# Splitting the tokens 256 and 288 in the output and down products, with one 512-column matmul for the high and low operand

## The reference

```python
def hybrid_layer(h, pos, states, p):
    u = rms_norm(h, p['norm_mix']) @ p['w_in']
    ...
    mixed = jnp.concatenate([y_ssd, y_ret, y_gla, y_lru], axis=-1) @ p['w_out']   # 1024 -> 1024
    h = h + mixed.astype(h.dtype)
    hn = rms_norm(h, p['norm_ffn'])
    h = h + ((jax.nn.silu(hn @ p['w_gate']) * (hn @ p['w_up'])) @ p['w_down']).astype(h.dtype)   # 2816 -> 1024
    return h, ...
```

## Time and profile before

| | |
|---|---|
| median of 3 runs | 1333.41 us |
| span of the profiled execution | 1330.0 us |
| TensorE matmul busy | 1298.5 us (98%), 10781 matmuls |
| TensorE weight load busy | 1248.2 us (94%), 10781 loads |
| VectorE busy | 856.3 us (64%) |
| ScalarE busy | 707.0 us (53%) |
| GpSimd busy | 293.9 us (22%) |

### The profile page before, as it was taken

One profiled execution on the slowest core, in us unless ns is written; L12 is line 12 of the kernel. 1 busy time (PEld: TensorE's weight loads), 2 busy tenths in 40 slices (PEclk: granted clock), 3 DMA queues, 4 the chain that ended last, 5 costly groups with the idle time before them and its releaser, 6 DMA issues.

```text
span 1330.0 us, 26928 instructions
## 1 busy us (share of the span) xinstructions
PE 1298.5 (98%) x10781; PEld 1248.2 (94%) x10781; DVE 856.3 (64%) x1697; ACT 707.0 (53%) x1209; POOL 293.9 (22%) x248
## 2 busy tenths in 40 slices
PE   7999999999999999999999999999999999999996
PEld 7988898999999999999998878889999999999996
DVE  5844766478853785378757547755788348834863
ACT  7625464666642674266663264556676247624641
POOL 1100100112243224324411010001123412341250
PEclk9999989999999999999999999999999999999997
DMA  8846745567744784476566566447477347835741
GB/s 269 212 102 143 163 109 122 109 143 166 173 129 104 171 170 128 104 171 170 145 143 156 114 151 160 96 113 161 103 170 188 111 104 169 190 109 104 169 125 68
DMA packets 63387, 189.73 MB, mean 143 GB/s; under 512 B 7584, under 2 KB 8864, under 8 KB 63264
## 3 DMA queue, kind: packets, MB, share of 16 engines
q0 software_dynamic: 27936, 67.12, 30.7%
q1 hardware_dynamic: 30672, 111.95, 26.7%
q10 hardware_dynamic: 4656, 8.95, 2.2%
HBM read 180.33 MB, written 5.43 MB: 140 GB/s over the span
## 4 chain that ended last, share of the span: by engine, by line
PE 79%; DVE 9%; ACT 4%; DVEq 3%; DMA 2%; issue 2%; ACTq 0%; SPq 0%
PE bank L1622 41%; PE bank L1651 31%; DVE ct L975 1%; DMA raw<-weights 1%; PE bank L1565 1%; DVE lru_x L975 1%; PE bank L1939 1%; ACT wl L540 1%; ACT wh L541 1%; DMA wl<-weights 1%; DVE up L1495 0%; PE bank L1583 0%; DVEq L974 0%; PE bank L1945 0%; DMA h<-x 0%
## 5 line engine op out<-in xcount | busy, mean ns | idle before, releaser
L512 POOL DMA_DIRECT2D wl<-weights x194 | 168.5, 869 | 892.4 <-ACT wl L540 880.3
L1622 PE MATMUL bank<-xh,wh 128*128 128x272 f32 x800 | 243.4, 304 | 8.1 <-DVE xl L930 7.7
L541 ACT ACTIVATE wh<-raw 128x512 fp32r<-128x512 f32 (+1 forms) x243 | 197.7, 815 | 89.0 <-PE bank L1622 79.2
L1622 PE MATMUL bank<-xh,wl 128*128 128x272 f32 x800 | 234.4, 293 | 0.0
L1622 PE MATMUL bank<-xl,wh 128*128 128x272 f32 x800 | 233.9, 292 | 0.0
L540 ACT ACTIVATE wl<-raw 128x512 fp32r<-128x512 f32 (+1 forms) x192 | 145.8, 759 | 126.1 <-PE bank L1622 114.2
L1651 PE MATMUL bank<-xh,wl 128*128 128x272 f32 x704 | 203.4, 289 | 0.0
L1651 PE MATMUL bank<-xh,wh 128*128 128x272 f32 x704 | 203.2, 289 | 0.2
L1651 PE MATMUL bank<-xl,wh 128*128 128x272 f32 x704 | 203.0, 288 | 0.0
L1622 PEld LDWEIGHTS bank<-xh,wh 128*128 128x128 f32 x800 | 154.2, 193 | 19.3 <-issue 17.4
L541 ACT ACTIVATE wh<-wsum 128x512 fp32r<-128x512 f32 x176 | 105.2, 622 | 124.1 <-DVE wsum L1392 83.7
(11 more groups left out here) (404 smaller groups left out, 3018.7 us busy)
## 6 DMA issues: line engine op xcount, KB each, us to landing
raw<-weights SPq DMA_DIRECT2D x202, 512.0 KB, 6.2
wl<-weights POOLq DMA_DIRECT2D x132, 256.0 KB, 5.5
wl<-weights POOLq DMA_DIRECT2D x62, 512.0 KB, 7.2
h<-x SPq DMA_DIRECT2D x4, 544.0 KB, 6.0
y<-h SPq DMA_DIRECT2D x4, 544.0 KB, 2.7
rv<-rk ACTq DMA_DIRECT2D x8, 136.0 KB, 2.5
tz<-rq ACTq DMA_DIRECT2D x8, 136.0 KB, 5.2
S<-s_ssd ACTq DMA_DIRECT2D x2, 512.0 KB, 6.5
```

What stands on the lines that cost most here:

```text
L512: nc.gpsimd.dma_start(wl[:, place(j)], weights[n][:, lo:lo + width], accum_op=ALU.add).then_inc(lo_added[BLOCK0[j] % RING], 16)
L541: a(wh[:, place(j)], whole, ACT.Copy).then_inc(hi_done, 1)
L1622: ins = mm(bank_, wt[:, at:at + P], xx[:, cols], start=(i == 0 and pass_ == 0), stop=(i == len(ks) - 1 and pass_ == 2))
```

## The change

For output and down units alone, the tokens are cut at 256 in place of 272: the first half-unit has 256 tokens, the second 288. In the first one, high and low operand now lie beside each other in one tensor (`g2`), and one matmul of 512 columns (2 x 256) runs both under one load of `wh`, into the two halves of the bank: columns 0 to 255 collect `wh` with the high operand, columns 256 to 511 `wh` with the low one. A second matmul of 256 columns adds `wl` with the high operand to the first 256 columns. So this half-unit has two matmuls per k in place of three. The second half-unit keeps three, of 288 columns. VectorE empties the first half-unit with two additions of 256 columns and a drain between them, since both change the same columns of `h`, and signals `dense_free` after the second. The columns streamed per k are 1632 before (6 x 272) and after (512 + 256 + 3 x 288).

```diff
+CUT = 256
+def split_in_two(q):
+    return q % 2 == 0 and q >= 2 * OUT0
+def half_cols(q):
+    cut = CUT if split_in_two(q - q % 2) else HALF
+    return slice(cut, TOK) if q % 2 else slice(0, cut)
...
-            gh[i], gl[i] = sb("gh_" + n, [2, TOK], F32R), sb("gl_" + n, [2, TOK], F32R)
+            g2[i] = sb("g_" + n, [2, 2, TOK], F32R)
+        gh, gl = [g[:, 0] for g in g2], [g[:, 1] for g in g2]
...
+        def operand_pair(k):
+            return g2[k // 2][:, :, k % 2, :]
...
                 def add_to_h(u, m):
-                    for half in range(2):
-                        acc, cols = take(u, half)
-                        ins = tt(h[:, m, cols], h[:, m, cols], acc, ALU.add)
-                        ins.then_inc(dense_free.sem, 1)
+
+                    acc, cols = take(u, 0)
+                    tt(h[:, m, cols], h[:, m, cols], acc[:, 0:CUT], ALU.add)
+                    dve.drain()
+                    tt(h[:, m, cols], h[:, m, cols], acc[:, CUT:2 * CUT], ALU.add).then_inc(dense_free.sem, 1)
+                    acc, cols = take(u, 1)
+                    tt(h[:, m, cols], h[:, m, cols], acc[:, 0:TOK - CUT], ALU.add).then_inc(dense_free.sem, 1)
...
-                    cols = slice(half * HALF, (half + 1) * HALF)
-                    bank_ = dense_bank(layer, q)
+                    cols = half_cols(q)
+                    whole = dense_bank(layer, q)
+                    bank_ = whole[:, 0:cols.stop - cols.start]
                     for i in steps:
                         if before is not None and half == 0:
                             before(i)
+                        at = place(j).start + i * P
+                        if split_in_two(q):
+                            x = operand_pair(ks[i])
+                            mm(stacked(whole[:], 2), wh[:, at:at + P], x[:, :, cols], start=i == 0, stop=False,
+                               skip_group_check=True)
+                            ins = mm(bank_, wl[:, at:at + P], x[:, 0, cols], start=False, stop=i == len(ks) - 1,
+                                     skip_group_check=True)
+                            continue
```

More of the change, by code:

```diff
@@ L313, in trunk @@
         early.close()
-        gh, gl = [None] * 4, [None] * 4
-        gh[G_RET], gl[G_RET] = sb("gh_ret", [2, TOK], F32R), sb("gl_ret", [2, TOK], F32R)
+        g2 = [None] * 4
+        g2[G_RET] = sb("g_ret", [2, 2, TOK], F32R)
         early = ExitStack()
@@ L427, in dense_bank @@
         def dense_bank(layer, q):
-            return (M[BORROWED[q]] if q in BORROWED else dense[(layer * (2 * NPLAIN) + q) % 3])[:, 0:HALF]
+            return M[BORROWED[q]] if q in BORROWED else dense[(layer * (2 * NPLAIN) + q) % 3]
         def norm_banks(i):
@@ L946, in take @@
                     dve.wait_ge(dense_done, layer * (2 * NPLAIN) + (q + 1))
-                    return dense_bank(layer, q), slice(half * HALF, (half + 1) * HALF)
+                    return dense_bank(layer, q), half_cols(q)
                 def conv(t, half):
@@ L952, in conv @@
                     acc, cols = take(u, half)
+                    acc = acc[:, 0:HALF]
                     row = cbuf[:, slot, :]
@@ L1618, in unit_half @@
                             before(i)
+                        at = place(j).start + i * P
[6 more added lines that the diff above has]
+                            continue
                         hi, lo = rhs(ks[i])
-                        at = place(j).start + i * P
                         for pass_, (wt, xx) in enumerate(((wh, hi), (wh, lo), (wl, hi))):
```

## The result

The changed kernel takes 1342.48 us, median of 4 runs (1341.0 to 1344.42); the kernel before took 1334.09 us beside it. The ratio is 1.0062, 95% interval 1.005 to 1.0075: 8.3 us slower. The forecast was 1336.8, +3.4 us, at most 1341.0; so the loss is more than twice the one forecast and the time lies outside the range.

The account below looks back on a forecast made before the run. The prediction took TensorE's matmul stream to bound the kernel. Its terms, -2.5 (stream) + 3.8 + 1.9 (holes) + 0.2 (later half-units) = +3.4 us, gave 1336.8 us, range 1329.0 to 1341.0.

Parts of the forecast that it names:

- The holes: Half-unit (2, 1) of each down group: TensorE waits longer for VectorE's additions, 3.8 us in four groups, 1.9 in two.
- The 0.2 us for later half-units of layer 0's last group: Down units, layer 0's last group: VectorE is full, so extra additions delay half-unit (4, 1); 0.2 us taken.
- The stream: TensorE in output and down units: 480 matmuls with their loads fewer, 5.2 ns saved per k, 2.5 us.
- The line through 512 and 272 columns: Matmul distance on TensorE: 0.444 ns per column plus 4.6 ns per matmul, giving 232, 118.3 and 132.5 ns.
- All per matmul: Rival for TensorE's output and down units: 5.9 us saved against 5.9 lost, 1333.4 us; chance 0.23.
- The load bounds the stream: Rival for output and down units: loads set 125 ns for 256 and 288 columns, net -10.9 us, 1322.5; chance 0.13.
- All per column: Rival for output and down units: the moving operand's read rate sets the time, nothing saved, +5.9 us, 1339.3; chance 0.22.
- So the time is the number of matmuls by their distance: Whole kernel: a change pays by shortening TensorE's stream or costs by putting a hole into it.
- More backlog: Rival: output units or layer 0's last group lose 2 us more, or two-piece operand streams slower, 1339 to 1343; chance 0.07.
- Output units at nothing: Output units: VectorE's extra additions end 0.5 to 0.8 us later but are covered, so costed at nothing.
- No gap at the squares: Behind the output units: the profile after would show no gap at the squares, the next wait on VectorE's chain.
- the cover of 1.25 us: Behind the output units: slack of 1.25 us before the squares at 294.66, to hide VectorE's later additions.

Follow-up runs that it names:

- e5: The changed kernel with half-unit (2, 1) of each down group in a bank of its own: 1337.07 us, ratio 1.0023 to the kernel before.
- e14: The changed kernel with lighter weight transfers in the gate and up stages: 1335.05 us, ratio 1.0012 to the kernel before.
- e15: The changed kernel without the second addition and the drain, with lighter gate and up weight transfers: 1329.05 us, ratio 0.9967 to the kernel before.
- e8: The changed kernel with the 512-column matmul issued as two of 256, each with its own load: 1342.34 us, ratio 1.0063 to the kernel before.
- e13: The kernel before with lighter weight transfers in the gate and up stages: 1330.46 us, ratio 0.9975 to the kernel before.
- e4: The kernel before with the change in the output units only: 1334.11 us, ratio 1.0002 to the kernel before.
- e3: The kernel before with the change in the down units only: 1338.45 us, ratio 1.0033 to the kernel before.
- e10: The kernel before with one product added twice in the first half of each of 48 down units: 1341.95 us, ratio 1.0048 to the kernel before.
- e1: The changed kernel without the second addition and the drain, low sum not added: 1335.17 us, ratio 1.0011 to the kernel before.
- e6: The change in the down units only, with half-unit (2, 1) in a bank of its own: 1335.47 us, ratio 1.001 to the kernel before.
- e16: The kernel before with 48 matmuls less in the down units and lighter gate and up transfers: 1328.27 us, ratio 0.9961 to the kernel before.
- e9: The kernel before with one matmul left out in the first half of each of 48 down units: 1331.9 us, ratio 0.9977 to the kernel before.

## Why the prediction was wrong

**The holes: right, in place and size.** Four times 0.94 and twice 0.97 were forecast. With the second matmul of (2, 1) counted, the first group has a gap of 997 + 239 ns after and of 126 + 170 before; less the streams of 118 + 133 and 126 + 125 that is 985 against 45, 0.94 us. In the last groups 1226 ns stand where 264 stood, 0.97 with the streams taken off. All six are within 0.01 us of each other by kind, and e5 gave 5.2 of the 5.7 us back. The 0.2 us for later half-units of layer 0's last group came to nothing in the changed kernel, for the reason given: TensorE arrives later too. Where it doesn't, in e5, the wait is there.

**The stream: right in kind, a little too big.** 5.2 ns per k were forecast and 3.4 measured, 480 x 3.4 = 1.6 us for 2.5. (The expectations for e14 and e15 have 4.0 and 1.9, from the 753 of the prediction; the trace of before has 752.5.) Layer 0's output stage shows the same: 48.06 us before, 47.84 after, for 64 k. The line through 512 and 272 columns was good (230, 118, 133 for 232, 118.3, 132.5). "All per matmul" and "The load bounds the stream" are out: 256 and 288 columns have different distances, and 352 of e8's 480 additional matmuls with their loads cost 1.6 us in the down stages, 4.5 ns each. "All per column" is out by the same 4.5 ns, though the saving lies under the 1.9 us from which the prediction let it decide. The Trainium skill ("TensorE: Matmul & The Clock Gate", section "Back-to-back issue gap") has N / 2.4 + 2.5 ns, and says that this is the gap of an isolated matmul and that in a stream of loads and matmuls 512 columns take about 131 ns. For this stream the trace agrees with neither: 230 ns for 512 columns, where the formula gives 215.8. The prediction used the formula for a stream.

**The step that failed is the one that turns the stream into time:** "So the time is the number of matmuls by their distance", and with it a sum in which only the stages that the change touches have terms. I read the 98% busy share and the one long wait as proof that everything between is full. It isn't: in the gate and up stages TensorE runs just at the edge of the weights' arrival. Here is the window over the first such stage of before and the down stage behind it (length, busy of PE, PEld, DVE, ACT, POOL, granted clock, share of the DMA engines, GB/s):

```profile
291.80:378.40 86.60, 86.03 (x676) 84.75 (x675) 72.79 (x121) 60.52 (x118) 22.34 (x23) 1.00 0.73 163
378.50:429.60 51.10, 51.10 (x410) 51.10 (x409) 17.64 (x29) 13.56 (x19) 18.41 (x10) 1.00 0.39 101
```

and of the changed kernel:

```profile
291.00:378.20 87.20, 85.86 (x676) 84.66 (x675) 73.21 (x122) 60.48 (x118) 22.17 (x23) 1.00 0.75 161
```

The same 676 matmuls take 0.6 us longer, with less of it busy, and the DMA engines at three quarters. The whole-kernel averages hide this, since a down stage needs only half that share. The term that was missing is +4.9 us of gate and up stages. With it, the wait in layer 1's output units (0.4) and a longer wait for `up` (0.2), the sum is -1.6 + 5.7 + 0.4 + 0.2 + 4.9 = +9.6; with -0.5 in the rest it is the 9.1 us by which the profiled executions differ, and the runs have 8.3. e13 against e14 shows that this term hangs on the transfers: 4.6 us of it by the stages, 3.4 by the runs. Both lighten the transfers of `raw` on the SP queue and those of `wl` on GpSimd's at once, so they don't tell which of the two it is.

The measured time lies in the range of the rival "More backlog" (1339 to 1343), but not for its reasons: the output units lose 0.4 us and layer 0's last group nothing beyond its hole, and the moving operand in two pieces streams as fast as in one.

**Output units at nothing: right in the time, wrong in the trace.** e4 measures +0.3 us, within 1.7 of nothing. But there is the wait at 943.32, and "No gap at the squares" was wrong further on: products of layer 1's gate stage wait behind the spreading of `rstd`, which came late (VectorE, loads, TensorE):

```profile
955.57 0.19 DVE L909 RECIPROCAL rstd<-rstd 128x5 f32<-128x5 f32 x1 [1.79 <-ACT rstd L615]
955.82 0.41 PEld L1589 LDWEIGHTS bank<-cx,rstd 128*128 128x128 f32 x4 [0.87 <-DVE rstd L909]
955.82 0.82 PE L1589 MATMUL bank<-cx,rstd 128*128 128x128 f32 x5 [0.65 <-DVE rstd L909]
```

The changed kernel, e4 and e5 have this wait (1.5 us of `rstd` in all against 0.8), e3, without the split in the output units, doesn't, and e14, with light transfers, doesn't either. So it takes both, the additions in the output units and the full transfers; how they combine isn't shown. I had worked out the cover of 1.25 us in layer 0 and taken it for both layers; it isn't safe in layer 0 either, where e4 waits 0.40 us for `rstd` at 300.69.

**Open.** Why the gate and up stages of before come out 3 to 6 us shorter than those of every kernel with another timing, more TensorE time (e10) as well as less (e9). That transfers carry it is shown; that the moments at which transfers meet in the queues decide it is only argued. Open too is why the runs of e1, e5 and e6 scatter more than all others, and why e16, with 48 matmuls less, is granted the full clock less of the time.

## What to carry to other kernels

A busy share of 97% doesn't say that time taken off that engine is time saved: ask for each stage what ends next to it, and take the share of the DMA engines stage by stage. Where a stage keeps pace with its transfers, a saving elsewhere can be worth less than its sum (3.1 of 6.0 us in e9) and a change of timing can cost there, and a cheap test is to lighten the transfers and see which stages shorten. Before one accumulator is split into two, count the signals that the next user of the bank waits for: here five additions in place of three at six places cost over three times what 480 fewer matmuls brought (5.7 us against 1.6).

## What was not expected of the hardware

- With full transfers the same gate and up instructions take 457.8 to 458.0 us in three executions of two kernels, and 460.7 to 463.6 us in eleven others; with light ones 455.0 to 455.8 in four kernels.
- A moving operand in two pieces of 256 columns (L1647) streams no slower than 512 columns in one: 230 ns to the next start in both the earlier trace rows. As two matmuls with two loads it takes 236.
- A profiled run's time is its span plus 1.8 us, in all 17 kernels where both are known (1342.05 and 1340.2). The kernel before's profiled execution (1330.0) was thus near 1331.8, one of its fastest. The 3.4 us that the prediction put between span and median are 1.8 that every run has and 1.6 by which this execution was faster than the median.
